# A gated-convolution layer with memory attention: attention moved into the last input round, output projection by 7-for-8 block products

## The reference

```python
h = rms_norm(x, pre_norm);  proj = h @ w_in          # 1024 x 5120
p, gate, mq = proj[..., :3072], proj[..., 3072:4608], proj[..., 4608:]
b_gate, c_gate, u = split(p, 3)
z = c_gate * u
mix = b_gate * (w0 * z[t-2] + w1 * z[t-1] + w2 * z[t])          # causal, 3 taps
kv = rms_norm(mem, mem_norm) @ w_mem_kv;  k, v = halves of kv   # 4 heads of 128
s = (mq . k) * 128 ** -0.5;  mem_o = softmax(s) . v             # 4 heads, 256 keys
y = (concat([mix, mem_o]) * silu(gate)) @ w_out                 # 1536 x 1024
out = x + rms_norm(y, post_norm)
```

## Time and profile before

| | before |
|---|---|
| median of 3 runs | 2371.03 us (2370.99 to 2372.04) |
| the profiled execution | 2373.23 us |
| its span, first to last instruction | 2371.5 us |
| TensorE busy, share of the span | 2237.3 us, 94% |
| VectorE | 1110.3 us, 47% |
| ScalarE | 711.0 us, 30% |
| mean granted TensorE clock | 0.975 |

### The profile page before, as it was taken

The page is one execution under the profiler, slowest core; times in us unless marked ns, Lnnn a source line. Parts: engine busy times, 40 slices in busy tenths (PEclk is TensorE's granted clock), DMA queues, the critical chain, the costliest instruction groups (busy, mean ns, idle before and its releaser), DMA issues.

```text
span 2371.5 us, 26241 instructions
## 1 busy us (share of the span) xinstructions
PE 2237.3 (94%) x10074; PEld 1851.6 (78%) x10074; DVE 1110.3 (47%) x1735; ACT 711.0 (30%) x1257; POOL 60.9 (3%) x108
## 2 busy tenths in 40 slices
PE   3899999999999999999999999997489999999997
PEld 2687878788888888888888888776378888888886
DVE  8577776713552243444351353231544444444531
ACT  4333433411211131221131121111444444444430
POOL 0000000000000000000000000000000000000000
PEclk9899999999999999999999999999599999999999
DMA  4686666777566677666577655547323333333321
GB/s 153 236 310 242 250 251 244 265 258 249 194 205 213 219 246 254 227 207 213 193 242 256 208 196 182 207 166 246 122 80 107 107 107 107 107 107 107 107 76 53
DMA packets 158235, 445.82 MB, mean 188 GB/s; under 512 B 13952, under 2 KB 46752, under 8 KB 155936
## 3 DMA queue, kind: packets, MB, share of 16 engines
q1 hardware_dynamic: 139984, 376.49, 46.3%
q0 software_dynamic: 18128, 67.66, 8.4%
HBM read 320.36 MB, written 123.73 MB: 187 GB/s over the span
## 4 chain that ended last, share of the span: by engine, by line
PE 85%; DVE 8%; DMA 3%; issue 2%; ACT 1%; SPq 0%; DVEq 0%; POOL 0%; ACTq 0%; POOLq 0%
PE banks L1162 28%; PE banks L1163 28%; PE banks L1164 28%; DVE hop_lo L811 2%; DMA slots<-w_split 2%; PE banks L1282 1%; DVE x_in L789 1%; DVE x_in L807 1%; DVE slots L841 1%; DMA q_raw<-q_kept 1%; DMA x_in<-in_x_t 0%; DVE wo_lo L1055 0%; DVE st_w L835 0%; DVE acc L784 0%; DMA conv_raw<-g_kept 0%
## 5 line engine op out<-in xcount | busy, mean ns | idle before, releaser
L1162 PE MATMUL banks<-hop_hi,slots 128*128 128x512 f32 x2240 | 882.7, 394 | 50.3 <-DVE hop_lo L811 22.3
L1163 PE MATMUL banks<-hop_lo,slots 128*128 128x512 f32 x2240 | 877.1, 392 | 0.0
L1164 PE MATMUL banks<-hop_hi,slots 128*128 128x512 f32 x2240 | 876.7, 391 | 0.0
L1162 PEld LDWEIGHTS banks<-hop_hi,slots 128*128 128x128 f32 x2240 | 424.0, 189 | 147.5 <-issue 43.7
L1164 PEld LDWEIGHTS banks<-hop_hi,slots 128*128 128x128 f32 x2240 | 423.8, 189 | 89.3
L1163 PEld LDWEIGHTS banks<-hop_lo,slots 128*128 128x128 f32 x2240 | 424.0, 189 | 88.7 <-issue 1.4
L1162 PE MATMUL banks<-wo_hi,gc_hi 128*128 128x512 f32 x512 | 202.6, 396 | 0.0
L1163 PE MATMUL banks<-wo_lo,gc_hi 128*128 128x512 f32 x512 | 199.9, 391 | 0.0
L1164 PE MATMUL banks<-wo_hi,gc_lo 128*128 128x512 f32 x512 | 199.7, 390 | 0.0
L886 DVE TENSOR_TENSOR u<-banks,u 128x512 f32<-128x512 f32 x56 | 38.7, 690 | 297.4 <-PE banks L1164 297.4
L579 ACT ACTIVATE s<-banks 128x512 f32<-128x512 f32 x80 | 47.8, 598 | 416.7 <-PE banks L1164 416.7
(11 more groups left out here) (137 smaller groups left out, 2344.7 us busy)
## 6 DMA issues: line engine op xcount, KB each, us to landing
slots<-w_split SPq DMA_DIRECT2D x420, 512.0 KB, 3.4
w_split<-slots SPq DMA_DIRECT2D x140, 512.0 KB, 2.9
raws<-in_w_in SPq DMA_DIRECT2D x80, 256.0 KB, 3.9
x_in<-in_x_t SPq DMA_DIRECT2D x16, 1024.0 KB, 6.9
g_kept<-mix POOLq DMA_DIRECT2D x16, 1024.0 KB, 6.6
x_res<-in_x POOLq DMA_DIRECT2D x32, 512.0 KB, 5.0
conv_raw<-g_kept SPq DMA_DIRECT2D x32, 512.0 KB, 4.6
out_x<-x_res POOLq DMA_DIRECT2D x32, 512.0 KB, 3.4
```

The lines of the kernel that those rows point to most:

```text
L1162: nc.tensor.matmul(dst, a, c, start=first, stop=False, skip_group_check=True)
L1163: nc.tensor.matmul(dst, a, d, start=False, stop=False, skip_group_check=True)
L1164: return nc.tensor.matmul(dst, b, c, start=False, stop=last, skip_group_check=True)
```

## The change

- *Round 3's order.* The two `q` pairs come first, then the other 18 (`LAST_ROWS`). Before, they were last.
- *Memory's keys and values* move to the start of round 3: norm in steps 6 to 15, the eight blocks after steps 17, 19, ... 31 (`KV_AT`), with two buffers for `w_kv` in place of one.
- *Attention* moves into round 3: head n is scored after step 33 + 80 n // 31 (`SCORE_AT`), so every 2 or 3 steps; `turn` stands three steps later and `weigh` four. `probs`, `q_raw`, `m_raw` get two buffers each. The gated heads go to DRAM (`mem_kept`) by GpSimd and come back later.
- *Output projection* becomes a fifth round (`OUT`). The convolution's rows of `w_out` (1024 x 1024) stand where x stood, as operands `hop_hi`, `hop_lo`; the gated tiles stand where weights stood, as units that are built on the fly, four steps ahead (raws from DRAM, ScalarE's upper half, VectorE's sums and lower half). There are 16 pairs of 2 x 128 tokens. Memory's 512 rows of `w_out` aren't done 7-for-8: units `M0` and `M1` hold a gated memory tile each and are multiplied with both halves of the columns (2 x 4 blocks of 3 matmuls for each unit), onto the same banks, or a bank of their own (`bank_m`) for one of the four blocks.
- *Norm and residual* of the output work on tiles in SBUF (`mix`) of 128 x 1024, with one square, one root, one scaling and one add per 128 tokens; three residual buffers in place of two.
- `g_kept` is laid out by 128-token tiles, so that a write has runs of 512 bytes where it had 2 KB, and each of the 16 writes becomes two of half the size.

The core of the diff, in the order of the file: constants, SyncE, `attention` of ScalarE, then of VectorE, and TensorE:

```diff
+LAST_ROWS = list(range(18, PAIRS)) + list(range(18))
+R1, R5, R6, R3, R7, R2, R4, M0, M1 = range(PRODUCTS + 2)
+FIRST_ORDER = [R1, R5, R6, R3, R7, R2, R4, M0, M1]
+OUT_ORDER = [R1, R5, R6, R3, M0, R7, R2, M1, R4]
+OUT_STEPS = [(ALL_PAIRS + j, r) for j in range(OUT_PAIRS) for r in (OUT_ORDER if j else FIRST_ORDER)]
+OUT_X_AT = {122: 0, 123: 1, 124: 3, 125: 2}
+OUT_RAW_AT = 127
-KV_AFTER = [3 * PAIRS + 10 + b for b in range(KV_BLOCKS)]
+KV_AT = [17 + 2 * b for b in range(KV_BLOCKS)]
+SCORE_AT = [33 + 80 * n // (HEADS - 1) for n in range(HEADS)]
+TURN_AT = [s + 3 for s in SCORE_AT]
+WEIGH_AT = [s + 4 for s in SCORE_AT]
...
+                        now = step - SLOTS
+                        if now == 2:
+                            sp.wait_ge(hop_lo_done, (m + 1) * PRODUCTS)
+                            sp.dma_start(mem_in[:], mem).then_inc(mem_dma, 16)
+                            load_kv(0)
+                            load_kv(1)
+                            load_q(0)
+                            load_q(1)
+                        if now in KV_AT and KV_AT.index(now) + 2 < KV_BLOCKS:
+                            load_kv(KV_AT.index(now) + 2)
...
+                        for n in range(HEADS):
+                            if n >= 2 and now == SCORE_AT[n - 2] + 1:
+                                load_q(n)
+                            if n >= 2 and now == WEIGH_AT[n - 2] + 1:
+                                load_m(n)
+                        if step in OUT_X_AT:
+                            sp.wait_ge(pv_done, HEADS)
+                            load_x(OUT_X_AT[step], OUT)
+                        if step == OUT_RAW_AT:
+                            sp.wait_ge(mem_gated, HEADS)
+                            for x in (X11, X21, X22, X12, G0, G1):
+                                load_raw(ALL_PAIRS, x)
...
+            def attention(step):
+                if step == SCORE_AT[0] - 1:
+                    query(0)
+                for n in range(HEADS):
+                    if step == TURN_AT[n] + 1:
+                        turned(n)
+                for n in range(HEADS):
+                    if step == SCORE_AT[n] + 1:
+                        if n + 1 < HEADS:
+                            query(n + 1)
+                        soften(n)
...
+            def attention(step):
+                if step == SCORE_AT[0] - 1:
+                    query(0)
+                for n in range(HEADS):
+                    if step == TURN_AT[n] + 1:
+                        turned(n)
+                for n in range(HEADS):
+                    if step == WEIGH_AT[n] + 1:
+                        gate(n)
+                    if step == SCORE_AT[n] + 1:
+                        row_maxima(n)
+                        if n + 1 < HEADS:
+                            query(n + 1)
+                for n in range(HEADS):
+                    if step == SCORE_AT[n] + 2:
+                        soften(n)
...
+            def add_memory(p, r):
+                unit_ready(UNIT_OF[p, r])
+                first = p == ALL_PAIRS
+                if r == M0:
+                    outputs = [(1, bank_x, False), (0, bank_b, not first)]
+                    pe.wait_ge(c11_done, p)
+                else:
+                    outputs = [(1, bank_m[p % 2], True), (0, bank_a[p % 2], False)]
...
+                for half, dst, start in outputs:
...
+                    for k in range(MH):
+                        g = [a[:, k * P:(k + 1) * P] for a in unit(UNIT_OF[p, r])]
+                        w = [a[:, k, :] for a in (WM_HI[half], WM_LO[half])]
+                        op = product(dst, g, w, start and k == 0, k == MH - 1)
...
             for p in range(ALL_PAIRS):
...
                     multiply(p, r)
...
+                        if step in KV_AT:
+                            keys_values(KV_AT.index(step))
+                        for n in range(HEADS):
+                            if step == TURN_AT[n]:
+                                turn(n)
+                            if step == SCORE_AT[n]:
+                                score(n)
+                        for n in range(HEADS):
+                            if step == WEIGH_AT[n]:
+                                weigh(n)
...
+            for n, (p, r) in enumerate(OUT_STEPS):
+                if r in (M0, M1):
+                    add_memory(p, r)
+                else:
+                    multiply(p, r)
```

On ScalarE and VectorE the steps of the output round stand in the same order. At the steps of its first pair, ScalarE also makes `hop_hi` of R4 and the upper halves of memory's weights (`WM_HI`), VectorE `hop_lo` of R2 and R4, a difference, and their lower halves (`WM_LO`); `finish` of the even 128-token tile stands after M1 and that of the odd one at R5 of the next pair:

```diff
+            for n, (p, r) in enumerate(OUT_STEPS):
+                j = p - ALL_PAIRS
+                if n == 0:
+                    use(ALL_PAIRS - 1, R4)
+                if n and OUT_STEPS[n - 1][1] == M1:
+                    finish(2 * (OUT_STEPS[n - 1][0] - ALL_PAIRS))
+                if r == R5 and j:
+                    finish(2 * j - 1)
...
+                if n == 0:
+                    operand_lo(OUT, R2)
+                    token_sum(OUT, 3)
+                if n == 1:
+                    operand_lo(OUT, R4)
+                ahead(OUT, n)
+                if n in (3, 4):
+                    half = n - 3
+                    dve.wait_ge(w_mem_hi, half + 1)
+                    dve.wait_ge(hop_lo_done, (OUT + 1) * PRODUCTS)
+                    nc.vector.tensor_tensor(WM_LO[half], (w_raw[:], Y22)[half], WM_HI[half].bitcast(f32),
+                                            ALU.subtract).then_inc(w_mem_lo, 1)
```

More of the change, by code:

```diff
@@ L1216, in multiply @@
                     pe.wait_ge(c22_done, p + 1)
+                starts = (R1, R5) if p > ALL_PAIRS else (R1, R5, R2)
                 for k in range(HK):
                     w = [a[:, k * P:(k + 1) * P] for a in unit(u)]
-                    op = product(dst, w, [a[:, r, k, :] for a in (hop_hi, hop_lo)], k == 0 and r in (R1, R5, R2), k == HK - 1)
+                    op = product(dst, w, [a[:, r, k, :] for a in (hop_hi, hop_lo)], k == 0 and r in starts, k == HK - 1)
                 op.then_inc(unit_done, 1)
@@ L1244, in turn_values, with score @@
                 op.then_inc(v_turned_done, 1)
+            def score(n):
+                h = n % MH
+                pe.wait_ge(q_lo_done, n + 1)
+                if n:
+                    pe.wait_ge(exp_done, n * SUB)
+                else:
+                    pe.wait_ge(kv_lo_done, KV_BLOCKS)
+                keys = [a[:, h, :] for a in (k_hi, k_lo)]
+                for s in range(SUB):
+                    op = product(scores[:, s, :], [a[:, s * P:(s + 1) * P] for a in (q_hi, q_lo)], keys, True, True)
+                op.then_inc(scores_done, 1)
@@ new lines, in turn, with weigh @@
+            def turn(n):
+                pe.wait_ge(probs_done, (n + 1) * SUB)
+                if n:
+                    pe.wait_ge(mem_gated, n)
+                for s in range(SUB):
+                    for a in range(MT):
+                        op = nc.tensor.transpose(probs_t[:, a, s * P:(s + 1) * P], probs[:, n % 2, s, a * P:(a + 1) * P], ident[:])
+                op.then_inc(turned_done, 1)
+            def weigh(n):
+                h = n % MH
+                pe.wait_ge(pt_lo_done, n + 1)
+                for a in range(MT):
+                    values = [u[:, a, h * HD:(h + 1) * HD] for u in (v_hi, v_lo)]
+                    op = product(mem_o, values, [u[:, a, :] for u in (pt_hi, pt_lo)], a == 0, a == MT - 1)
+                op.then_inc(pv_done, 1)
@@ L1257, in _ @@
                                 sum_tokens(2 * (m + 1) + half)
-                    elif step == 55:
-                        sum_tokens(NT, NM)
-                    if p - 1 in KV_AFTER and r == R5 and KV_AFTER.index(p - 1) >= MH:
-                        turn_values(KV_AFTER.index(p - 1))
-                if p in KV_AFTER:
-                    keys_values(KV_AFTER.index(p))
-            def score(n):
-                h = n % MH
-                pe.wait_ge(q_lo_done, n + 1)
-                if n:
-                    pe.wait_ge(exp_done, n * SUB)
-                keys = [a[:, h, :] for a in (k_hi, k_lo)]
-                for s in range(SUB):
-                    op = product(scores[:, s, :], [a[:, s * P:(s + 1) * P] for a in (q_hi, q_lo)], keys, True, True)
-                op.then_inc(scores_done, 1)
@@ L1311, in _ @@
-            pe.wait_ge(kv_lo_done, KV_BLOCKS)
-            for step in range(-9, 8 * NT):
-                if step % 2:
-                    if 0 <= (step + 7) // 2 < NT * MH:
-                        weigh((step + 7) // 2)
-                    if 0 <= (step + 9) // 2 < NT * MH:
-                        score((step + 9) // 2)
-                elif 0 <= (step + 8) // 2 < NT * MH:
-                    turn((step + 8) // 2)
-                if step >= 0:
-                    group(step)
+                    else:
+                        if step == 11:
+                            sum_tokens(NT, NM)
+                        if step - 1 in KV_AT and KV_AT.index(step - 1) >= MH:
+                            turn_values(KV_AT.index(step - 1))
+                        if step in KV_AT:
[5 more added lines that the diff above has]
```

(4 more changed lines are left out.)

871 lines of the change are left out of this document (434 added, 437 removed).

## The result

The changed kernel takes 2275.43 us (median of 4 runs, 2273.77 to 2279.64) against 2371.53 for the kernel before in the same runs: ratio 0.9593, 95% interval 0.9574 to 0.9611, so 4.1% faster. I had said 2282. Its profiled execution, the slowest of the four, has a span of 2277.8 us.

A forecast was written before the change was run, and what follows sets the result against it. TensorE was taken to bound every stage but the lead-in and the tail. 2371.5 - 713.0 + 121.6 + 478.8 + 13 - 6.5 + 5 + 10 + 1 + 1 = 2282.4 us, forecast as 2282, range 2260 to 2322.

The forecast's parts named there:

- TensorE's pace decides: Whole kernel: time is number of matmuls times 0.227 us plus exposed waits; output products 478.8 us in place of 522.3.
- Attention at 3.8 us a head: Attention's matmuls, only moved into round 3: 3.8 us a head, 121.6 us for 32 heads.
- The lead-in goes: Between round 3 and the first output group: the lead-in of 86.8 us is removed.
- Attention's waits: Round 3: weigh waits for late pt_lo after short gaps, 10 us; far bound 76.
- short gaps: Round 3: 13 heads followed after two products expose pt_lo waits of about 0.75 us each, ScalarE being behind.
- Bursts: Round 3, SyncE's queue: two bursts of loads delay units, 3 us and 2 us; bounds 0 and 12 together.
- rival 3: The DMA engines bind: 512 B writes and bursts hold unit loads back, 38 + 12 in place of 6, 2326 us; chance 0.07.
- Keys and values: Round 3: waits after the eight blocks fall from 9.5 to 3 us, -6.5; bounds 0 and 12.
- The entry: Entry to the output round: VectorE's work delays units, 11 us, plus 2 for a lowered clock, 13; bounds 2 and 22.
- Pieces of 512 B: Writes of gated tiles in 512-byte runs cost 1 us over 16 writes; far bound 38.
- Everything hidden: Entry costs 2, attention's waits 2, bursts, small pieces, keys and values 0: 2254 us; chance 0.13.
- Rivals 2 and 4: Attention: weigh waits 2.37 us at each head, 2348 us, chance 0.14; turn waits for its probabilities, slower, 2507 us, chance 0.05.

The follow-up runs named there:

- e1: Changed kernel with the first product (R1) of every output-round pair issued twice, 8 products in place of 7: 2316.42 us.
- e8: Changed kernel without attention (scores, softmax, transposes, weighing and loads of q left out; the gate squares m): 2148.66 us.
- e12: Kernel before the change, without attention (scores, softmax, transposes, weighing and loads of q left out; the gate squares m): 2230.96 us.
- e4: Changed kernel with a head scored every 2 products throughout, in place of every 2 or 3: 2276.70 us.
- e7: Changed kernel with heads' steps chosen so no short gap puts the next head's exponentials in a step with a SiLU or convolution: 2273.32 us.
- e3: Changed kernel with the two w_kv blocks and two q tiles at round 3's start loaded at later steps, mem where it was: 2269.83 us.
- e5: Changed kernel with the output's weight loads in round 3 every third step in place of every step, first gated tiles at step 134: 2273.14 us.
- e6: Changed kernel with only the order of ScalarE's, VectorE's and TensorE's work at the entry to the output round changed: 2275.52 us.
- e10: Changed kernel with the edits of e3, e5, e6 and e7 together: 2260.85 us.
- e9: e6 with the four products of the last g pair with its gate moved from VectorE to GpSimd: 2277.03 us.
- e2: Changed kernel with the burst of loads at round 3's start issued one unit load later: 2273.33 us.

## Why the prediction held, point by point

- *TensorE's pace decides.* Right. The output round took 486.9 us with its entry; behind the first pair, from 1814.5 (1800.85, a product of 2.72 and 48 matmuls) to 2263.4, 15 pairs take 29.9 us each, as I said. e1 gives 42.2 of 43.5 us for the product saved.
- *Attention at 3.8 us a head.* 32 heads cost 125.9 us in round 3 (e8), 3.9 a head with all waits, where I had 121.6 + 10. Of it, from the distances between starts in the trace, 118.3 are matmuls.
- *The lead-in goes.* Right; e12 splits its 87 us.
- *Attention's waits*, 10 us: measured 4.8. The step of the short gaps failed in its mechanism: "ScalarE is just then behind the next head's exponentials" is no wait by itself (e4); it takes a table load or a convolution in the same step (e7). I had named a SiLU's table load and a convolution as the larger cases, 1.5 us, and charged the gap besides.
- *Bursts*, 3 + 2 us: 4.6 + 1.9 of waits, and 2.3 and 1.6 us of half clock after them, 10.4 in all, near the 12 that rival 3 gave them. The mechanism was right (e3, e5), the first term too small: the burst began only at 1241.40, behind SyncE's wait for `hop_lo`, and the unit behind it was wanted at 1248.09 (1252.70 less the wait), 6.7 us later and not 10.9.
- *Keys and values*, 3 us: 1.2.
- *The entry*, 13 us: 1.75 at the last product of round 3, then 5.4, and 1.6 of half clock, 8.8 in all. That VectorE's work sets it is supported by e6, where the longest wait, 2.51 us, is for VectorE's `slots` at the fifth product, as forecast. In the changed kernel itself the sign failed: no wait of the entry is for slots or hop_lo, and the longest, 2.55, is for ScalarE's `s` at the third product. My list of VectorE's instructions, each added to the one before, came out too long by some 4 us.
- *Pieces of 512 B*, 1 us: nothing seen. Rounds 1 and 2 have no wait for a unit; the product behind the wait for `u` in round 3 starts at 1236.9 to 1239.7 in the twelve profiled executions with the new writes, at 1238.3 in that of the kernel before. The Trainium skill (DMA: Bandwidth & Descriptors, Specifications) gives 512 bytes as the least size for line rate. No run here shows that: a write of 1 MB landed 6.6 us after its issue before, its two halves 8.0 us after the first one's issue now (medians); nothing waited for them. The far bound of 38 was far off.
- *Rivals.* Everything hidden (2254) didn't come, but e10, with most of it hidden, reaches 2261. Rivals 2 and 4 are out: no wait at the turn, no waits over 2 us in attention, a granted clock of 0.99 in round 3. Of rival 3 only the part of the bursts came true, the 10.4 us above. "None over 3 us" was wrong, by one wait of 4.6. "Near 540 us" for round 3 was a slip: my own terms give 418.1 + 121.6 - 6.5 + 5 + 10 + 1 = 549.2, and 548.4 were measured.
- *Luck.* The sum lies 4.6 us over the profiled span partly because its errors ran both ways: the bursts cost 5.4 us more than I had, the entry 4.2, attention with its waits and half clock 4.1 and keys and values 1.8 less.

The sum of what was found, on spans: -43.5 for the product, -15.6 for attention (e8, e12), -37.3 for the output's operands (46.1 less the entry's 8.8), -8.3 for keys and values, +10.4 for the two bursts (6.5 of waits, 3.9 of half clock), +1.6 for half clock in attention, +1.4 ahead of round 3, +0.7 in the tail: -90.6 of the measured -93.7. The 3 us between are as large as what single executions differ by.

## What to carry to other kernels

When one engine binds everywhere but in one stretch, moving that stretch's work into a stage with short, steady matmul groups is worth its idle time, here 53 us of 94: 16 from the long chains (softmax, transposes), 37 from loading and splitting the next stage's operands under matmuls. Another 43.5 came from issuing fewer matmuls, and loads issued in bursts took 10 back. Cost chains by what else stands in order on the same engine in that very step (a table load, a convolution), not by the distance between steps. And spread loads that are needed late: two bursts of 2.6 and 5.8 MB cost more than all of attention's waits.

## What the runs showed of the hardware

- A wait of about 2 us lowers TensorE's clock in one execution and not in another. After the wait of 2.55 us the clock was whole for five matmuls, then half for eight (starts 0.43 us apart in place of 0.227), 1.6 us lost:

```profile
1785.92 0.39 PE L1286 MATMUL banks<-hop_lo,slots 128*128 128x512 f32 x1
...
1786.14 0.59 PE L1287 MATMUL banks<-hop_hi,slots 128*128 128x512 f32 x1
...
1786.96 0.63 PE L1286 MATMUL banks<-hop_lo,slots 128*128 128x512 f32 x1
...
1787.38 0.63 PE L1287 MATMUL banks<-hop_hi,slots 128*128 128x512 f32 x1
```

  After the wait of 1.79 us the same happened in the profiled executions of the changed kernel, e3 and e9 and not in those of e1, e2, e5 and e6; after that of 1.85 us in those of the changed kernel, e4 and e7 and not in e1, e2, e3, e6 and e9. It costs 1.2 to 1.8 us each time, and a single profile is uncertain by as much. Behind the first burst's wait of 3.4 to 4.8 us a stretch of half clock came in each of the nine profiled executions that have that wait.
- A VectorE instruction with two SBUF operands took 1.36 us in place of 0.69 beside one of GpSimd of 1.29 us. The Trainium skill (SBUF — State Buffer, SBUF: two separate sides) has such a VectorE instruction and a GpSimd one that reads SBUF lock each other out for whole instructions; the trace agrees, as VectorE's ended 0.55 us after GpSimd's end at 1771.37. It holds the other way too: the last of the four gates, started at 1778.28 beside VectorE's `hop_lo` (1777.24 to 1779.52), took GpSimd 2.39 us.
